# Attention's first pair of heads: who makes the near low parts, and where two softplus steps stand in ScalarE's queue

## What is computed

```python
z = q @ k.T * scale + bias                    # t: query, s: key
log_keep = where(s < t, log_sigmoid(-z), 0)   # = -softplus(z) where the key is older
after = cumsum(log_keep, reversed) - log_keep
att = where(s < t, exp(log_sigmoid(z) + after), 0)
o = att @ v
```

## Time and profile before

| | us |
|---|---|
| median of 3 runs | 2593.91 |
| lowest, highest | 2592.84, 2600.52 |
| the profiled execution | 2593.98 |
| its span | 2591.7 |

### The profile page before, as it was taken

One profiled execution on the slowest core, in us unless ns is written; L12 is line 12 of the kernel. 1 busy time (PEld: TensorE's weight loads), 2 busy tenths in 40 slices (PEclk: granted clock), 3 DMA queues, 4 the chain that ended last, 5 costly groups with the idle time before them and its releaser, 6 DMA issues.

```text
span 2591.7 us, 52186 instructions
## 1 busy us (share of the span) xinstructions
PE 2535.2 (98%) x21955; PEld 2447.2 (94%) x21955; DVE 1301.4 (50%) x1739; ACT 916.4 (35%) x1384; POOL 281.3 (11%) x348
## 2 busy tenths in 40 slices
PE   8999999999999999999999999999999999999998
PEld 7999999998888899999999999999986699999998
DVE  4434346765655554343464344434556754344454
ACT  4222234454323432222353232222348842222244
POOL 2000002001223200000120000000243220000021
PEclk9999999999999999999999999999999999999999
DMA  5223222221011332323222433232303423232331
GB/s 147 84 81 97 82 85 93 97 82 32 20 36 45 109 96 81 97 81 97 85 94 82 126 120 97 81 97 77 111 25 114 147 82 91 88 90 89 93 98 58
DMA packets 308138, 225.96 MB, mean 87 GB/s; under 512 B 8270, under 2 KB 301567, under 8 KB 307967
## 3 DMA queue, kind: packets, MB, share of 16 engines
q1 hardware_dynamic: 307280, 224.26, 28.6%
q0 software_dynamic: 576, 0.00, 0.0%
q10 hardware_dynamic: 162, 0.04, 0.0%
HBM read 212.14 MB, written 12.13 MB: 87 GB/s over the span
## 4 chain that ended last, share of the span: by engine, by line
PE 94%; DVE 3%; issue 1%; ACT 1%; DMA 1%; POOL 0%; SPq 0%; DVEq 0%; POOLq 0%; ACTq 0%
PE ps L551 79%; PE ps L2460 1%; PE ps L2426 1%; PE ps L570 1%; PE ps L1824 1%; PE ps L1828 1%; PE ps L2365 1%; PE ps L2468 1%; PE ps L1572 0%; PE ps L2626 0%; PE ps L2462 0%; PE ps L2463 0%; PE ps L1835 0%; PE ps L1659 0%; PE ps L1767 0%
## 5 line engine op out<-in xcount | busy, mean ns | idle before, releaser
L551 PE MATMUL ps<-hx_hi,w_hi 128*128 128x288 f32 x3730 | 1070.6, 287 | 1.6 <-DVE hx_lo L2581 0.6
L551 PE MATMUL ps<-hx_lo,w_hi 128*128 128x288 f32 x3730 | 1066.8, 286 | 0.0
L551 PE MATMUL ps<-hx_hi,w_lo 128*128 128x288 f32 x3730 | 1066.8, 286 | 0.0
L488 ACT ACTIVATE w_hi<-raw 128x1024 fp32r<-128x1024 f32 (+1 forms) x362 | 374.5, 1035 | 1207.4 <-PE ps L551 1202.7
L551 PEld LDWEIGHTS ps<-hx_hi,w_hi 128*128 128x128 f32 x3730 | 704.9, 189 | 4.7 <-issue 2.5
L551 PEld LDWEIGHTS ps<-hx_lo,w_hi 128*128 128x128 f32 x3730 | 705.0, 189 | 0.3
L551 PEld LDWEIGHTS ps<-hx_hi,w_lo 128*128 128x128 f32 x3730 | 705.0, 189 | 0.0
L551 PE MATMUL ps<-hid_hi,w_hi 128*128 128x288 f32 x1888 | 543.2, 288 | 0.6 <-DVE hid_lo L1528 0.5
L551 PE MATMUL ps<-hid_lo,w_hi 128*128 128x288 f32 x1888 | 541.4, 287 | 0.0
L551 PE MATMUL ps<-hid_hi,w_lo 128*128 128x288 f32 x1888 | 541.4, 287 | 0.0
L503 DVE TENSOR_TENSOR w_lo<-raw,w_hi 128x1024 fp32r<-128x1024 f32 (+1 forms) x362 | 436.8, 1207 | 111.2 <-ACT w_hi L488 111.1
(11 more groups left out here) (483 smaller groups left out, 2279.7 us busy)
## 6 DMA issues: line engine op xcount, KB each, us to landing
raw<-in_ffn_w_in SPq DMA_DIRECT2D x176, 512.0 KB, 4.9
raw<-in_ffn_w_out SPq DMA_DIRECT2D x64, 512.0 KB, 4.1
raw<-in_a_w_in SPq DMA_DIRECT2D x33, 512.0 KB, 4.5
raw<-in_ffn_w_out SPq DMA_DIRECT2D x32, 384.0 KB, 3.5
raw<-in_ple_w_gate SPq DMA_DIRECT2D x8, 1024.0 KB, 5.1
raw<-in_w_kv SPq DMA_DIRECT2D x16, 512.0 KB, 4.1
k_page<-in_cache_k SPq DMA_DIRECT2D x16, 512.0 KB, 3.6
v_page<-in_cache_v SPq DMA_DIRECT2D x14, 512.0 KB, 4.8
```

Source lines behind the costliest of these rows:

```text
L488: nc.scalar.activation(w_hi[:, m, 0:k], s.view(m, slot), ACT.Copy).then_inc(w_hi_done, 1)
L551: last = nc.tensor.matmul(TILE[m][:, c0:c1], w[:, m, k], columns(h, k, c0, c1), start=k == 0 and a == 0, stop=k == k_all - 1 and a == 2)
```

## The change

In the first pair, three near low parts move from GpSimd to VectorE, right behind the near maxima. Far maxima come next on VectorE, and the new tokens' bias and cap behind them. On ScalarE, near high parts stand ahead of the far logarithms; the far high parts and the new tokens' exp and log move behind the near weights of pair 0, ahead of the exponentials of pair 1. GpSimd waits for VectorE's three low parts before it makes the two far ones. The warm-up matmuls before the first sums are 14, not 28.

```diff
--- before.py
+++ after.py
@@ -2026,7 +2026,7 @@
                 nc.gpsimd.tensor_copy(q_blocks[rows_, :, a], qT[rows_, :, TP:T].rearrange("p f (b t) -> p f b t", t=TD)
                                       ).then_inc(at["q_sample"], 1)
             pool.wait_ge(at["q_sample"], 2)
-            low_parts(0, BANK_B + (BANK_C,), 0)
+            pool.wait_ge(at["lo"], 3)
             low_parts(0, BANK_A, 3)
             pool.wait_ge(at["lo"], 5)
             after(pool, "keepn")
@@ -2105,13 +2105,8 @@
             exps(0, BANK_B + (BANK_C,), 0)
             lns(0, BANK_B + (BANK_C,), 0)
             exps(0, BANK_A, 3)
+            high_parts(0, BANK_B + (BANK_C,), 0)
             lns(0, BANK_A, 3)
-            high_parts(0, BANK_B + (BANK_C,), 0)
-            high_parts(0, BANK_A, 3)
-            after(act, "zcn")
-            done("en", nc.scalar.activation(ls_new[:], ls_new[:], ACT.Exp))
-            after(act, "en")
-            done("ln", nc.scalar.activation(ls_new[:], ls_new[:], ACT.Ln, bias=1.0))
             for n in range(NP):
                 weights(n, 1, BANK_C, 0, QC)
                 weights(n, 1, BANK_C + QC, 1, QC).then_inc(at["att"], 1)
@@ -2119,6 +2114,12 @@
                     weights(n, 2 + a, BANK_B[a], a, 512).then_inc(at["att"], 1)
                 if n == NP - 1:
                     break
+                if not n:
+                    high_parts(n, BANK_A, 3)
+                    after(act, "zcn")
+                    done("en", nc.scalar.activation(ls_new[:], ls_new[:], ACT.Exp))
+                    after(act, "en")
+                    done("ln", nc.scalar.activation(ls_new[:], ls_new[:], ACT.Ln, bias=1.0))
                 if n:
                     high_parts(n, BANK_A, 3)
                     k_copy(n, 0)
@@ -2259,12 +2260,16 @@
             near(capped, 0, at["zc"])
             far(capped, 0, at["zc"])
             near(softplus, 0, at["max"])
+            for g, first in enumerate(BANK_B + (BANK_C,)):
+                dve.wait_ge(at["hi"], g + 1)
+                tt(bank_of(ls_lo[:, 0], first), bank_of(ls[:, 0], first), bank_of(ls_hi[:, 0], first).bitcast(F32), ALU.subtract
+                   ).then_inc(at["lo"], 1)
+            far(softplus, 0, at["max"])
             after(dve, "zn")
             zn = ps[0:TS, 6:8].rearrange("p c (h x) -> p (c h) x", x=TS)
             done("zbn", tt(zb_new[:], zn, lowered(bias_b[0:TS], TS), ALU.add))
             after(dve, "zbn")
             done("zcn", nc.vector.tensor_scalar(ls_new[:], zb_new[:], SOFTPLUS_CAP, None, ALU.min))
-            far(softplus, 0, at["max"])
             after(dve, "ln")
             done("maxn", tt(ls_new[:], ls_new[:], zb_new[:], ALU.max))
             after(dve, "maxn")
@@ -2475,7 +2480,7 @@
             far_scores(0)
             new_scores()
             pe.wait_ge(at["made"], 5)
-            keep_warm(pe, 28, O_BANK)
+            keep_warm(pe, 14, O_BANK)
             for n in range(NP):
                 pe.wait_ge(at["lo"], 5 * n + 3)
                 sums(n, 0, 2)
```

## The result

| | before | changed |
|---|---|---|
| median | 2594.19 us (20 runs) | 2601.11 us (20 runs) |
| lowest to highest | 2588.18 to 2600.52 | 2596.0 to 2606.53 |
| the profiled execution | 2593.98 us, span 2591.7 | 2597.69 us, span 2596.0 |
| ratio, 95% interval | | 1.0025 (1.0017 to 1.0032) |

The changed kernel is slower by a quarter of a percent, 6.5 us by the ratio. The forecast was 2596.8 us, and the median lies 1.1 us above the end of its range.

A forecast was written before the change was run, and what follows sets the result against it. The prediction took TensorE to bound the kernel, with 94% of the chain. From 2593.98 us, sums -3.4, far_scores(1) +3.4, new_outputs +0.9 and clock +1.9 gave 2596.8 us, range 2591.6 to 2600.0.

The forecast's parts named there:

- Near low parts on VectorE: Pair 0's three low parts on VectorE let TensorE's near sums start at about 1917.4 us, 3.4 us earlier.
- The log 3.4 us later, maxn, keepn and maskn at 1.2 us each: ScalarE's new-token log ends 3.4 us later; the three VectorE steps behind it take 3.6 us together.
- All of the gain given back at far_scores(1): TensorE waits 3.3 us for pair 1's far weights, losing the whole 3.4 us gain.
- New_outputs 0.9 us late through attn: TensorE's new_outputs waits for attn and starts at 1935.9 us, not 1935.00.
- The clock falls in the new idle: TensorE's 3.3 us idle before far_scores(1) lowers its clock from 2.4 to 1.2 GHz, about 7 in 10.
- Its price: Half clock in far_scores(1) and new_outputs costs 1.9 us, with bounds 0.5 and 3.2 us.
- The sum: Whole kernel: -3.4, +3.4, +0.9 and +1.9 us on 2593.98 give 2596.8 us, bounds 2595.3 and 2598.1.
- The gain that stays: Rival: far weights and attn are in time despite the late log, so 2590.6 us; chance 0.08.
- the kept clock: Rival: same waits in pair 0 but TensorE's clock stays up, so 2594.9 us; chance 0.23.
- the totals' stretch falls away: Rival: the totals no longer lower the clock, saving 3.1 us, so 2591.8 us; chance 0.13.
- The long half clock: Rival: the clock stays low from the new idle until pair 1, 2598.2 us; chance 0.06 for beyond 0.3% slower.

The follow-up runs named there:

- fill3: Changed kernel with 3 unused matmuls of 512 float32 columns ahead of TensorE's wait for pair 0's far weights: 2596.88 us, ratio 1.0012.
- mask: Changed kernel with maskn moved ahead of VectorE's wait for the new tokens' log: 2598.86 us, ratio 1.0018.
- late_only: Kernel before with only the far high parts and the new tokens' exp and log moved behind the near weights: 2602.23 us, a single run.
- warm28: Changed kernel with 28 warm-up matmuls again, not 14: 2601.01 us, a single run.
- low_only: Changed kernel with far high parts and the new tokens' exp and log back ahead of the near weights: 2598.33 us, ratio 1.0013.
- best: Changed kernel, maskn and pair 1's caps ahead of the log wait, GpSimd's small transfers ahead of far low parts, half the totals moved later: 2593.76 us.
- caps_warm: Changed kernel, maskn and pair 1's caps ahead of the log wait, nine unused 384-column matmuls between and in the totals: 2594.66 us, ratio 0.9994.
- fill: Changed kernel with 13 unused matmuls of 512 float32 columns ahead of TensorE's wait for pair 0's far weights: 2604.55 us, ratio 1.0040.

## Why the prediction was wrong, step by step

- **Near low parts on VectorE: right.** 1.90 us for three, 0.63 us apart; I had 0.60 us. The sums started 9.92 us after the first scores, where 1917.4 us in the old trace is 9.9.
- **The log 3.4 us later, maxn, keepn and maskn at 1.2 us each: right.** 1.22, 1.22 and 1.21 us. GpSimd was done at 1923.44 us, 0.09 us after maxn had started, so the two hardly met. That their old 1.92 and 2.19 us came from GpSimd's subtractions was an argument from the earlier trace rows; the changed kernel's rows, with GpSimd done, bear it out. They agree with the exclusion that the Trainium skill states in SBUF — State Buffer, Who interferes with whom; the 0.1 us that maxn would have waited by that rule does not show, since maxn took as long as keepn.
- **All of the gain given back at far_scores(1): right.** Forecast: an idle of 3.3 us and a start 0.08 us later than before. Measured: 3.24 us and 0.06 us.
- **New_outputs 0.9 us late through attn: right as a wait**, seen bare in fill3 (idle 0.75 us, start 0.88 us late). In the changed kernel no idle is left there, since far_scores(1) at half clock ran past attn's end (1934.67 us).
- **The clock falls in the new idle: right.** I gave it 7 in 10 and it fell in each of the six traces with an idle of 2.1 us or more. One of its reasons was weaker than I took it for: the idle of 1.64 us near 704 us, which the prediction read in before, stands in all fourteen traces, and the low clock followed within 2 us in five of them, the first trace of before among them, and not in the nine others. The Trainium skill, TensorE: Matmul & The Clock Gate, section HAM oscillation, which I also named, gives its rule for idles longer than the 3.3 us forecast here, so it spoke for the fall less than I made of it.
- **Its price: the step that failed.** I set 1.9 us, at most 3.2 us, for far_scores(1) and new_outputs. Measured against fill3, the same waits without the low clock: 2.4 us up to the key transposes, 2.9 us up to the totals, 3.6 us up to pair 1's sums. Against fill3's whole attention it is 5.1 us, but not all of that belongs to the new idle: fill3 also had 3.4 us less of low clock at the totals (0.9 us up to pair 2's near scores) and none at the end (1.3 us from there on). For these two places the prediction had no term: it left the totals' stretch as it was and had nothing at attention's end. The rate was right: far_scores(1) took 2.08 us for 1.13, new_outputs 3.78 us for 2.05. The length was wrong. I let the stretch end behind new_outputs, while it held 10.24 us, and with it the far weighing (the changed kernel's last step ahead of the transposes) and the first transposes (1.12 us, 0.65 before). I took the 6.83 us at half clock in before for the upper bound although nothing sets one, and the same trace has a longer stretch, ahead of attention:

```profile
860.95:871.19 10.24, 10.24 (x40) 9.06 (x40) 10.16 (x19) 4.94 (x7) 0.00 (x0) 0.50 0.31 104
```

- **The sum.** Against the first trace of before: 0.06 us at far_scores(1), 1.2 and 1.7 us of half speed in it and in new_outputs, the rest in the far weighing, the transposes and the totals: 4.2 us, and 1.0 us at the end; 5.3 us where I had 2.8. Two slips in the bounds change nothing: 6.83 x 0.45 is 3.1 us, not 3.2, and 2593.98 + 0.9 + 0.5 is 2595.4. The median's 6.9 us holds 1 to 2 us more, which is within the interval, and which no trace places.
- **Rivals.** The gain that stays and the kept clock are refuted by both traces. That the totals' stretch falls away did not happen. The long half clock, which had 0.06, was the nearest in kind, and its own sum of 2598.2 us the nearest in size (2593.98 + 5.3 is 2599.3 us): mask, late_only and warm28 show it at 20.5 to 23.9 us in one piece, and in the changed kernel only 3.4 us at full clock stand between the two stretches.

## What to carry to other kernels

An earlier start is worth nothing until the next wait is named: write down for each of the bounding engine's steps how early its inputs were, and look what an in-order queue holds behind a step that is moved late; here three instructions and then the next pair's caps stood behind one log. Where a change leaves the bounding TensorE idle for some two microseconds, price the clock over the work that follows, further than the next step (here 10 to 24 us of low clock), and try a kernel that fills the idle: it parts the wait from the clock in one run. Compare marks counted from the stage's own start when two kernels differ by less than equal kernels do.

## What the runs showed of the hardware

All six idles of 2.10 us and more were followed by 1.2 GHz, and how long it stayed there did not follow the idle's length: behind 2.10 us (mask) it was 20.48 us, behind 3.23 us (late_only and warm28) 23.89 us, behind 3.24 and 3.23 us (the changed kernel's two traces) 10.24 us, behind 4.13 us (low_only) 10.24 us. A shorter idle did not decide it: the one of 1.64 us, which all fourteen traces have near 702 us, was followed by the low clock within 2 us in five of them and not in nine. In late_only TensorE was busy for 23.73 of the 23.89 us and the clock did not come back. The Trainium skill, TensorE: Matmul & The Clock Gate, Part 1, says that activity releases the throttle; here busy time in the profile did not for that long, and what did release it the runs don't tell. TensorE's rows show no idle in the totals either, the matmuls of one column (L2373 in before, 1939.14 to 1943.94 us), and wherever the clock was at 2.4 GHz when they began, it fell during them or, in best and caps_warm, up to 2.2 us behind their first half. In before it fell at 1942.96 us:

```profile
1939.14 1.94 PE L2373 MATMUL ps<-ones,new_cols 64*128 64x1 f32 x16
1941.01 0.66 PE L2365 MATMUL ps<-ident,k_page 128*128 128x128 f32 x4
1941.60 2.34 PE L2373 MATMUL ps<-ones,new_cols 64*128 64x1 f32 x16
```

A float32 matmul of 512 columns with 128 rows took 0.87 us in two records (fill), against 0.24 us for the same columns in fp32r in the warm-up.
